# Layers of the second block: mixing, second and most of the first feed-forward product with seven half-size products for eight, gated rows turned by TensorE

## The reference, cut to what matters

```
for l in range(2):
    proj = h @ w_in                      # retention, pooling and forgetting-attention inputs
    mix  = concat([retention, pool, attention]) @ w_out          # 1024 x 1024
    h    = layer_norm(ALPHA * h + mix)
    a, b = h @ w1, h @ w3                                        # 1024 x 2816 each
    y    = (silu(a) * b) @ w2                                    # 2816 x 1024
    h    = layer_norm(ALPHA * h + y)
```

## Time and profile before

| | |
|---|---|
| median of 3 runs | 3254.3 us (3250.01 to 3260.01) |
| span of the profiled execution | 3252.7 us; no time of its own is given beside the span |
| the two layers of the second block | about 1900 to 3252 us of the span |
| mean granted TensorE clock | 0.973 |
| PE busy | 3120.2 us, 96% |
| DVE, ACT, POOL busy | 975.8, 540.8 and 47.2 us |

### The profile page before, as it was taken

One profiled execution on the slowest core, in us unless ns is written; L12 is line 12 of the kernel. 1 busy time (PEld: TensorE's weight loads), 2 busy tenths in 40 slices (PEclk: granted clock), 3 DMA queues, 4 the chain that ended last, 5 costly groups with the idle time before them and its releaser, 6 DMA issues.

```text
span 3252.7 us, 52666 instructions
## 1 busy us (share of the span) xinstructions
PE 3120.2 (96%) x22631; PEld 1747.5 (54%) x22631; DVE 975.8 (30%) x2146; ACT 540.8 (17%) x1129; POOL 47.2 (1%) x58
## 2 busy tenths in 40 slices
PE   9878989999999999999999999999999999999999
PEld 3355545333343333333345668574785758675866
DVE  1633455232223223222363431223023122132101
ACT  1332311111111111111122220130102100040000
POOL 0000002000000000000010000000000000000000
PEclk9888979999999999999989999999999999999999
DMA  9800115999999999999863333234333243243532
GB/s 400 354 1 27 53 53 224 386 410 403 408 397 406 400 406 407 407 407 404 351 251 119 125 130 117 111 143 176 135 126 142 105 194 133 100 176 116 195 145 100
DMA packets 97466, 743.70 MB, mean 229 GB/s; under 512 B 11128, under 2 KB 38336, under 8 KB 57552
## 3 DMA queue, kind: packets, MB, share of 16 engines
q1 hardware_dynamic: 58768, 687.49, 53.6%
q10 hardware_dynamic: 32624, 30.52, 2.9%
q0 software_dynamic: 5968, 24.14, 1.9%
HBM read 674.98 MB, written 67.13 MB: 228 GB/s over the span
## 4 chain that ended last, share of the span: by engine, by line
PE 55%; DMA 28%; DVE 3%; ACT 2%; issue 1%; ACTq 1%; POOL 0%; DVEq 0%
DMA arena<-x_sorted 27%; PE psum L1593 19%; PE psum L1610 9%; PE psum L1540 5%; PE psum L1579 3%; PE psum L1551 3%; PE psum L1244 1%; PE psum L802 1%; ACTq L587 1%; PE psum L1355 1%; PE psum L820 1%; PE psum L1196 1%; PE psum L1319 1%; PE psum L1411 1%; PE psum L1457 1%
## 5 line engine op out<-in xcount | busy, mean ns | idle before, releaser
L1244 PE MATMUL psum<-weight_ring,arena 128*32 128x512 f32 x6192 | 680.8, 594 | 23.6 <-DVE arena L2862 21.7
L1593 PE MATMUL psum<-arena,weight_ring 128*128 128x256 f32 (+1 forms) x2816 | 632.2, 383 | 3.1 <-ACT arena L2226 3.1
L1593 PEld LDWEIGHTS psum<-arena,weight_ring 128*128 128x128 f32 x2816 | 527.6, 189 | 99.0 <-issue 11.0
L1244 PEld LDWEIGHTS psum<-weight_ring,arena 128*32 128x32 f32 x6192 | 199.7, 110 | 485.5 <-issue 464.3
L1319 PE MATMUL psum<-weight_ring,arena 128*32 128x256 f32 x6144 | 338.2, 380 | 0.0
L1610 PE MATMUL psum<-weight_ring 128*128 128x512 f32 x704 | 305.4, 593 | 4.2 <-DVE weight_ring L3149 4.2
L1319 PEld LDWEIGHTS psum<-weight_ring,arena 128*32 128x32 f32 x6144 | 196.6, 110 | 153.0 <-issue 26.8
L1610 PEld LDWEIGHTS psum<-weight_ring 128*128 128x128 f32 x704 | 132.9, 190 | 169.3 <-issue 162.5
L2884 DVE STREAM_TRANSPOSE arena<-arena 128x384 f32<-128x384 f32 x32 | 18.6, 580 | 630.8 <-DMA arena<-x_sorted 630.8
L3149 DVE TENSOR_TENSOR weight_ring<-weight_ring,psum 128x256 f32<-128x256 f32 (+1 forms) x88 | 37.5, 426 | 486.1 <-PE psum L1593 480.3
L1540 PE MATMUL psum<-weight_ring,arena 128*128 128x512 f32 (+2 forms) x512 | 170.0, 489 | 3.1 <-ACT arena L2226 3.1
(11 more groups left out here) (435 smaller groups left out, 2532.0 us busy)
## 6 DMA issues: line engine op xcount, KB each, us to landing
weight_ring<-exp_gu SPq DMA_DIRECT2D x129, 2048.0 KB, 11.9
weight_ring<-weights SPq DMA_DIRECT2D x104, 2048.0 KB, 7.8
weight_ring<-exp_down SPq DMA_DIRECT2D x64, 2048.0 KB, 11.5
x_sorted<-arena SPq DMA_DIRECT2D x2, 10752.0 KB
arena<-x_sorted ACTq DMA_DIRECT2D x132, 96.0 KB, 21.6
y_sorted<-arena ACTq DMA_DIRECT2D x128, 96.0 KB, 17.6
y_sorted<-arena SPq DMA_DIRECT2D x2, 5632.0 KB, 39.7
y_sorted<-arena SPq DMA_DIRECT2D x2, 5120.0 KB, 37.3
```

The source lines that it names most:

```text
L1244: mm = pe.matmul(psum[j * GROUP:(j + 1) * GROUP, g, :], xg[:, k // 4, g, k % 4 * GROUP:(k % 4 + 1) * GROUP], w[:, kk, j * 512:(j + 1) * 51 ...
L1593: mm = pe.matmul(bank[:, 0:b - a], w[:, k, col:col + P], h2_t[:, k, a:b], start=(k == 0), stop=(k == KT - 1))
```

## The change

Three kinds of product are cut into 2 x 2 blocks and made with seven block products instead of eight (the Winograd form): `mix` of (0, B), (1, A), (1, B); the second product of features tiles 0 to 15, in two chunks of 8, for all four halves; and the first product of features tiles 0 to 19 for (0, B), (1, A), (1, B), in five pieces of 4 tiles. One such product is a **unit**: rows in two tiles of 128 (`t`, `first`), the contraction in two parts, the columns in two parts of 512 (for the first product 512 gate columns and 512 of the other factor). Each block product is 4 matmuls of 512 columns. There are 26 units: 15 up, 8 down, 3 mix. Third chunk (tiles 16 to 21) of the second product, (0, A)'s first product and (0, A)'s mix stay as they were in kind (`plain`).

What a unit needs beside the products, with the names of the code and the blocks b11, b12 (first half of the depth), b21, b22 of the weights:

- POOL: `fast_t1 = b12 - b11` (128x2048), and `b12 = b22 - b12` in place, in two parts of 1024.
- DVE: `b11 = b22 - fast_t1` in place (`third_difference`, 128x2048), `b21 = b21 - b11` (128x2048), where a chunk opens four sums of row blocks `fast_s1` to `fast_s4` (128x512 each), and additions of the products out of PSUM. An up unit has seven 128x512 operations after the differences.
- In up units results are rows x features, so that TensorE has to transpose the gated rows (`turn_hidden`, 8 transposes of 128x128 a unit) and ACT copies them to `ff_t` (`hidden_copied`); they are turned in the middle of the next unit.
- Attention steps stand at fixed slots: before products 1, 5... as `STEP_SLOTS` says, four in an up unit, two in a down unit.
- Both pieces of weights of a unit are given free together at its end.

```diff
+FAST_MIX = [(0, "B"), (1, "A"), (1, "B")]
+FAST_CHUNKS = (0, 1)
+FAST_UP = ((0, "B"), (1, "A"), (1, "B"))
+UP_UNITS = ((0, 1), (2, 3), (4,))
+STEP_SLOTS = dict(mix=(), down=(2, 5), up=(0, 2, 4, 6))
...
-FF_CHUNKS = ((0, 12), (12, FT))
+FF_CHUNKS = ((0, 8), (8, 16), (16, FT))
...
+            def fast(u, piece, steps, ready, ready_late):
...
+                def product_1():
+                    product(main.open(pe, bx), lambda k: rows(k, t), b11).then_inc(part_filled, 1)
+
+                def product_5():
+                    bank = main.open(pe, by)
+                    pe.wait_ge(sums_ready, count_at(sums_of, u, "s1" if opens_chunk(u) else "t2"))
+                    pe.wait_ge(diffs_ready, 3 * u + 1)
+                    product(bank, lambda k: fast_s1[:, k, :], fast_t1).then_inc(part_filled, 1)
...
+                step(0)
+                product_1()
...
+                if turning is None:
+                    step(1)
+                    product_5()
+                    step(2)
+                    product_2()
+                elif name == "up":
+                    turn_hidden(turning, "t", bz)
+                    product_5()
+                    turn_hidden(turning, "first", bz)
+                    step(2)
+                    product_2()
+                else:
+                    step(2)
+                    turn_hidden(turning, "t", bz)
+                    turn_hidden(turning, "first", by)
+                    pe.wait_ge(*main.drained_of(("turned", turning, "t")))
+                    product_2()
+                    product_5()
+                step(3)
+                bank_6 = main.open(pe, bz)
+                pe.wait_ge(sums_ready, count_at(sums_of, u, "t2"))
...
+                mm = product(bank_6, lambda k: fast_s2[:, k, :], b11)
+                main.ship(mm, ("fast", u, "p6"), "v", bz)
+                step(4)
...
+                product(bank_7, lambda k: s3[:, k, :] if s3 is not None else rows(k, first), b12).then_inc(part_filled, 1)
+                step(5)
+                pe.wait_ge(sums_ready, count_at(sums_of, u, "v"))
+                mm = product(main.psum[:, by, :], lambda k: fast_s4[:, k, :], b22, False)
...
+                step(6)
+                pe.wait_ge(sums_ready, count_at(sums_of, u, "c22"))
+                mm = product(bank_7, lambda k: rows(depth + k, first), b21, False)
+                main.ship(mm, ("fast", u, "c21"), "v", bx)
+                piece_free[at_a] = piece_free[at_b] = main.done()
...
+                for part in (slice(0, depth // 2), slice(depth // 2, depth)):
+                    pool.tensor_tensor(b12[:, part, :], b22[:, part, :], b12[:, part, :], ALU.subtract).then_inc(diffs_ready, 1)
...
+                def third_difference():
+                    at_b = fast_at[u][1]
+                    dve.wait_ge(layer_landed[at_b % LAYER_SLOTS], layer_count(at_b))
+                    dve.wait_ge(diffs_ready, 3 * u + 1)
+                    dve.wait_ge(part_filled, 3 * u + 1)
+                    then(dve.tensor_tensor(b11, b22, t1, ALU.subtract), sums_ready)
...
+                if turning is None and opens_chunk(u):
+                    sums()
+                step(0)
+                if opens_chunk(u) and turning is not None:
+                    step(2)
+                    dve.wait_ge(*main.drained_of(("turned", turning, "t")))
+                    dve.wait_ge(*main.drained_of(("turned", turning, "first")))
+                    sums()
+                    third_difference()
+                else:
+                    third_difference()
+                    if turning is None:
+                        step(1)
+                    step(2)
...
+                fourth_difference()
```

More of the change, by code:

```diff
@@ L1616, in feed_down, with ready @@
[L1616 to L1617 removed]
+                hidden = [FAST.index(unit) for unit in ups(l, x, c)]
+                key = ("down", l, x, c)
+                def ready():
+                    for u in hidden:
+                        if key not in FAST or u != waits_turn(FAST.index(key)):
+                            for tile in ("t", "first"):
+                                pe.wait_ge(*main.drained_of(("turned", u, tile)))
+                    if not hidden or c == LAST_CHUNK:
+                        pe.wait_ge(*main.drained_of(("up", l, x, f1 - 1)))
@@ new lines, in add, with meta_added @@
+            def add(tile, half, other, factor, done=None):
+                part = h2[:, tile, half * 512:(half + 1) * 512]
+                V.did(dve.scalar_tensor_tensor(part, part, factor, other, ALU.mult, ALU.add), done)
+            def meta_added(key, factor):
+                bank = main.take(dve, key)
+                for j in range(4):
+                    part = h2[0:META, 0, j * 256:(j + 1) * 256]
+                    V.did(dve.scalar_tensor_tensor(part, part, factor, bank[32 * j:32 * j + META, 0:256], ALU.mult, ALU.add),
+                          main.drained["v"] if j == 3 else None)
```

593 lines of the change are left out of this document (458 added, 135 removed).

## The result

| | before | after |
|---|---|---|
| median of 4 runs | 3254.6 us | 3282.2 us |
| lowest, highest | 3250.0, 3260.0 us | 3277.9, 3287.3 us |
| span of the profiled execution | 3252.7 us | 3276.7 us |

The account below looks back on a forecast made before the run. TensorE's own work, busy 96% of the span, was taken as the bound. From 3254.3 us, 75.7 us of saved work came off and 40.5 us of new waits were added: 3219 us, range 3186 to 3248.

Parts of the forecast that it names:

- The work saved: TensorE: seven products for eight save 52.7 us in up units, 38.0 in down and mix; transposes add 15; net 75.7.
- DVE beside POOL: Feed units: contention left out of the sum, named only in a rival as up to 8.4 us of DVE a unit.
- DVE becomes the bound: Rival, 16 feed units beside attention steps: DVE's load makes it slower, 3267 to 3299 us; chance 0.07 together with late weights.
- late weights: Rival: loads or POOL late, 26 units lose some 3 us, 78 us; slower share 0.07 together with DVE's load.
- Place 1: Product 5 of up units that open no chunk waits for the third difference: 18.9 us together.
- The clock behind waits: TensorE in the layers: clock expected at 1.00; a gap bringing the 1.2 GHz level would cost more than its length; unsized.
- Places 2 to 4: Waits at the norm step 3 us, softmax steps 12, down units behind up units 3.6, mix units 3.
- The norm step: Place 2, (1, A)'s norm step in (0, B)'s third up unit: 9.0 us of DVE, 3 us of wait.
- The turned rows: Place 4, six down units behind up units: product 2 waits 0.60 us for the rows' copy, 3.6 us together.
- place 3: Softmax steps beside second down units and (1, A)'s last up unit: 12 us of waits together.
- The mix units: Three mix units: sums ahead of product 5 cost about 1 us each, 3 us in the sum.
- POOL's duration: POOL's difference of 2048 elements: 2.1 us from below, 4.2 us as upper bound, 8.4 us a unit, taken as hidden.

Follow-up runs that it names:

- e1: Changed kernel with POOL's three differences covering 8 of 512 columns, every wait kept; ratio 0.9939 to the kernel before, layers 1465.2 us.
- f1: Changed kernel with both e1's thin POOL differences and e2's removed wait; ratio 0.9868 to the kernel before, layers 1439.7 us.
- f4: Changed kernel with each POOL difference cut into instructions of 128 x 256; ratio 0.9983 to the kernel before, layers 1471.8 us.
- i1: Changed kernel with POOL's three differences replaced by copies of the same shapes; ratio 0.9971 to the kernel before, layers 1468.4 us.
- e2: Changed kernel without product 5's wait for the third difference in up units opening no chunk; ratio 0.9998 to the kernel before, layers 1485.3 us.
- g1: Changed kernel with every unit plain, keeping three chunks, new layout and smaller DMA scratch; ratio 1.0032 to the kernel before, layers 1488.8 us.
- g3: Changed kernel with f4's pieces, e2's removed wait and (0, B)'s mix plain; ratio 0.9905 to the kernel before, layers 1442.4 us.
- h2: g3 with a DMA scratch of 2560 in place of 2048; ratio 0.9864 to the kernel before, 3220.1 us, layers 1439.0 us.

## Why the prediction was wrong

Forecast 3219 us, measured 3282: 63 us too few. 54 of them are in the layers (-35.2 forecast, +18.8 measured), 9 outside them. Of the 54, e1 puts 39.9 on POOL's work beside DVE and leaves 14.1, of which the clock behind waits is the main term.

- **The work saved**: right. 0.432 us a record, 24.2 us for 28 products; no run contradicts 75.7 us. With waits and clock removed as far as f1 does, 46.6 of it are in the layers' length, and f1's remaining waits and slowed products (29.2 us) make up the rest.
- **DVE beside POOL, put at nothing: the step that failed.** The passage that takes "the upper, 8.4 us a unit" for POOL and then works out its cover asked only whether TensorE waits for POOL. It doesn't: no row of its waits names POOL. But POOL's 10 us a unit (4.69 + 2 x 2.68 us) stop DVE, and TensorE waits for that. e1 puts it at 39.9 us; f4 and i1 show the mechanism. It was the rival "DVE becomes the bound", which decides from 35 us beyond the 40.5; 39.9 + 14.1 = 54 us came. I gave it, together with late weights, 0.07. The rows could not have shown the lock, as POOL was idle in the layers, but a loss of up to 8.4 us a unit stood in the text as its bound and was left out of the sum and of the range, which ended at 3248.
- **Place 1**: forecast 18.9 us, measured 18.8 in six waits (2.09 in (1, B) for 1.9, 6.21 behind the norm step for 5.9, 4.22 in (0, B) for 4.4, and 2.09 in (1, A) for 2.9). The chain was right, and POOL doesn't touch it: e1 has the same 18.8. The wait wasn't needed at all: product 5 doesn't read what it waits for, and e2 gives 20 us back.
- **The clock behind waits, named but put at nothing: the second step that failed.** 20.9 us in eleven products behind waits of the changed kernel and 2.9 in two behind late transposes, 15.7 in eight of e1's.
- **Places 2 to 4**: forecast 21.6 us; e1's new waits of these kinds are 19.1, near it by luck. The norm step has 2.0 for 3. The turned rows have 9.5 for 3.6, but 5.3 of it in one wait in (1, A) behind softmax steps, where place 3 had about 4. The mix units have 7.6 (5.36 in (0, B), 2.24 in (1, A)) for 3. The 8 us of place 3 before product 5 of the second down units don't show in e1 at all; in the changed kernel, beside POOL, (0, A) has 4.4.
- **e1 as a test of the whole sum**: -75.7 + 54.6 = -21.1 us. Of 54.6, 37.5 are waits (48.7 less the 11.2 of before), 15.7 clock, 2.5 third chunk and layout (g1), together 1.1 too many. The forecast of 40.5 had the waits 3 us too large and lacked the other two.
- **POOL's duration**: 4.2 us forecast as upper bound for 2048 elements, 4.51 measured; two inputs cost more than twice a copy (1.90 us in i1). DVE's 2.28 us: 2.29 measured.
- **Weights late**: no; transfers landed in a median of 7.9 us for 7.8, and no product waited for one.

## What to carry to other kernels

Work laid on POOL beside a busy DVE isn't priced by whether somebody waits for POOL, but by how long each POOL instruction keeps DVE's two-input instructions waiting, and who waits for DVE; cutting it into short instructions gave back 33 of 40 us here. A wait should name what the instruction reads: product 5's wait on a later semaphore count cost 20 us. And a gap of 2.1 us in a stretch of dense products cost 3.8 us in 10 of 16 cases (place 1 in the changed kernel, e1, f4 and i1), since the product behind it began at the 1.2 GHz level, and just its 2.1 us in the other 6: bound the clock with the waits, not apart from them.

## What the runs showed of the hardware

- A DVE operation on 192 elements, two inputs from SBUF, lasted 4.68 us beside a POOL subtraction of 4.51 us, 2.05 us beside a copy of 1.90 us, 0.90 us beside pieces of 0.85 us, and 0.35 us alone. With one input in PSUM, additions of 512 elements stayed within 673 to 692 ns (L3504 and L3604), 15 of them while POOL subtracted.
- POOL is held up as well: a subtraction of 2048 elements that began 1.1 us into a DVE difference of 2.28 us lasted 5.55 us for 4.51 (2816.64 in the changed kernel); the mean of all 26 is 4.69 us.
- The clock behind a gap is not settled by the gap's length: the product behind the same 3.07 us lasted 5.40 us in g3 and 3.70 us in h2.
- With a DMA scratch of 2048, the 15th of 16 scatters in a row waited 6.5 to 28.1 us; with 2560 or the default it waited 0.3.
